# Chunk inverses of the first layer: one compact 64x64 tile per head in place of block-diagonal pairs

## The chip, the cores and the metric

The kernel runs on one core of a Trainium2 chip. The metric is the device time of one execution in microseconds. Three runs of the kernel before took 1829.59 to 1830.82 us, with a median of 1830.16 us.

## What is computed

The reference is a trunk of two layers on 256 tokens of width 1024. Layer 0 runs an RWKV-7 time mixer (8 heads of 64, both directions) beside an attention mixer, projects, and ends in a dense SwiGLU. Layer 1 runs a gated linear attention and a top-2-of-8 mixture of experts. The change touches only the recurrence of the RWKV-7 mixer:

```python
def step(state, inp):
    r_t, w_t, k_t, v_t, a_t, b_t = inp
    sa = jnp.einsum('bhvk,bhk->bhv', state, a_t)
    new = state * w_t[:, :, None, :] + sa[..., None] * b_t[:, :, None, :] + v_t[..., None] * k_t[:, :, None, :]
    read = state if reverse else new
    return new, jnp.einsum('bhvk,bhk->bhv', read, r_t)
...
_, out = lax.scan(step, init, xs, reverse=reverse)
```

The kernel does this scan in chunks of 64 tokens. In a chunk the `sa` of all tokens solve a triangular system of 64 unknowns for each head and direction; with its inverse at hand, the rest of the chunk is a few 64x64 products.

## The kernel before

All activations lie transposed, features on the partitions. 128 partitions hold two heads of 64 features (h = 0, 1); four such tiles (t, `RT` = 4) hold the eight heads, and two directions (d) double them. So each of the `NCH` = 4 steps of the chunk loop handles 16 systems, the list `SYSTEMS`; direction 0 takes chunk s and direction 1 chunk 3-s. The whole stage is one block of three engine programs (TensorE, ScalarE, VectorE) that order themselves by semaphores; SyncE issues nothing in it. Each engine executes its own list in the order in which it is written.

The steps are taken in pairs (s, s+1). The two members of a pair have a slot each (q = 0, 1) with its own tiles, and a pair goes through three parts.

- **Grams** (`grams`, L778 to L795, twice). TensorE forms for each of the 16 systems the products of decayed keys, values and queries in banks 0 to 4, and turns B, K and (first pair only) V into banks 5 to 7. VectorE masks bank 0 into X (L928), adds the identity (L935), forms XT from MT (L937, L938), and masks RB, AK and RK (L932, six instructions of 128x256). ScalarE copies MT (L883) and the turned tiles (L886). `grams(s+1)` may write a bank only once it has been taken from for step s.
- **Levels** (`levels`, L803 through `pairs_product`). The inverse of a unit triangular 64x64 matrix is built by doubling: X holds the inverse of the diagonal blocks of size b and XT its transpose; each of the five levels b = 2, 4, 8, 16, 32 multiplies M by X, masks the product with the level's mask (`masked_product`, L908), multiplies the masked product by X from either side, and adds what comes out to X and XT (`add_pairs`, L914). On the last level only XT is needed.
- **Recurrence** (`recur`, L832 to L854, twice): W, U, the new state and the output of the step, each a product of 64x64 per system, with copies by ScalarE (L890, L892) and sums by VectorE (L901, L903, L965 to L968).

In the levels, X, XT, MT and the masked product are stored as 8 tiles of 128x128: tile (d, t) has head 0's matrix in its upper left 64x64 block, head 1's in the lower right one, and zeros elsewhere. One matmul of 128x128 by 128 columns multiplies both heads at once. A product of a slot is 8 matmuls into two banks (one for each direction), and each VectorE pass over it takes two instructions of 128x512 elements. The zeros are written once, by two memsets of 128x3072 at the start of the block (L919); the first MT copy and VectorE itself wait for them. Since the blocks are written one head at a time, the X mask takes two instructions of 64x512 and the MT copy four of 64x256.

Within a level the written order is, on TensorE: M times X of slot 0, of slot 1, then both second products of slot 0, both of slot 1. On VectorE: mask of slot 0, mask of slot 1, adds of slot 0, adds of slot 1. A matmul of f32 operands leaves two MATMUL records (and two LDWEIGHTS records) in the trace, so that the 448 matmuls of `pairs_product` count as 896.

The block before this one ends at about 162 us with the attention mixer, the one behind it (L979 on) begins at about 347 us with the group norm and the output projection.

Of the kernel before, what the change touches and what calls it, by code (L numbers as in the profile page):

```python
# [7 lines left out]
P = 128  # L8
KT = D // P
TT = S // P  # L10
HD = 64
RW = 512
RT = RW // P
C = 64
# [73 lines left out]
def program(nc, io):  # L88
# [13 lines left out]
    with ctx:  # L102
# [590 lines left out]
        for q in range(2):  # L693
            at = TEMP_ + q * 3 * 1024
            slots.append({n: area(at + 1024 * j, 8, 2 * C) for j, n in enumerate(("X", "XT", "MT"))})
            at = TEMP_ + 8192 + q * 6 * 512
            slots[q].update({n: tile8(at + 512 * j) for j, n in enumerate(("AK", "RB", "RK", "Bt", "Kt", "Vt"))})
        product = [area(TEMP_ + 6144, 8, 2 * C), area(TEMP_ + 7168, 8, 2 * C)]
# [17 lines left out]
        def head_blocks(v, h):  # L716

            return v[HD * h:HD * (h + 1), :, C * h:C * (h + 1)]

# [5 lines left out]

        def by_direction(v):

            return v.rearrange("p (d t) (h n) -> p d (t h) n", d=2, h=2)

        def both_heads(name):  # L730
            return cst(name).rearrange("p (d n) -> p d n", d=2).unsqueeze(2).to_broadcast([P, 2, 2 * RT, C])

# [18 lines left out]
        eye = ident.unsqueeze(1).to_broadcast([P, 8, 2 * C])  # L751
        zeroed = sem("zeroed")

        with nc.Block(no_gpsimd_drain=True) as block:
            @block.tensor
            def _(pe):
# [42 lines left out]
                def pairs_product(bank, left, right):  # L799

                    for d in range(2):
                        for t in range(RT):
                            last = nc.tensor.matmul(ps[bank + d][:, t * 2 * C:(t + 1) * 2 * C], left[:, RT * d + t], right[:, RT * d + t],  # L803
                                                    start=True, stop=True)
                    return last

                def levels(s):
                    pe.wait_ge(grams_taken_dve, 4 * (s + 2))
                    pe.wait_ge(grams_taken_act, act_groups(s + 2))
                    for n in range(1, len(LEVELS)):  # L810
                        done = len(LEVELS) * (s // 2)
                        for q in range(2):
                            o = slots[q]
                            pe.wait_ge(inverse_ready[q], done + n)
                            pairs_product(4 * q, o["MT"], o["X"]).then_inc(product_ready[q], 1)
                        for q in range(2):
                            o = slots[q]
                            pe.wait_ge(product_masked[q], (len(LEVELS) - 1) * (s // 2) + n)
                            last = pairs_product(4 * q + 2, product[q], o["XT"])
                            if n < len(LEVELS) - 1:  # L820
                                last = pairs_product(4 * q, o["XT"], product[q])
                            last.then_inc(blocks_ready[q], 1)

                def recur(s):
# [11 lines left out]
                    for d, t, h in SYSTEMS:  # L836
                        p, j = slice(HD * h, HD * (h + 1)), RT * d + t
                        last = nc.tensor.matmul(bank8(5)[p, j], o["XT"][p, j, C * h:C * (h + 1)], W[p, j], start=True, stop=True)
# [29 lines left out]
            def _(act):  # L868
                for s in range(0, NCH, 2):
                    for q in range(2):  # L870
                        o = slots[q]
                        for n, (name, bank) in enumerate((("MT", 1), ("Bt", 5), ("Kt", 6), ("Vt", 7))):
# [3 lines left out]
                            if name == "MT":  # L876
                                act.wait_ge(grams_ready, gram_groups(s + q) + 3)
                                if s + q < 1:
                                    act.wait_ge(zeroed, 2)
                                for d in range(2):  # L880
                                    for h in range(2):
                                        rows = slice(HD * h, HD * (h + 1))
                                        last = nc.scalar.activation(head_blocks(o[name], h)[:, RT * d:RT * (d + 1)],  # L883
                                                                    side_by_side(1 + d)[rows, :, 0], ACT.Copy)
# [10 lines left out]
            def _(dve):  # L895
# [10 lines left out]
                def masked_product(q, d, name):  # L906
                    mask = cst(name)[:, d * C:(d + 1) * C].unsqueeze(1).to_broadcast([P, 2 * RT, C])
                    return nc.vector.tensor_tensor(product[q][:, RT * d:RT * (d + 1)].rearrange("p t (h n) -> p (t h) n", h=2),  # L908
                                                   bank8(4 * q + d), mask, mul)

                def add_pairs(v, bank):
                    for d in range(2):
# [1160 lines left out]
```

## Time and profile before

| | |
|---|---|
| median of three runs | 1830.16 us |
| profiled execution: span from the first to the last instruction | 1828.1 us |
| TensorE busy, whole span | 1694.6 us (93%) |
| VectorE busy, whole span | 1370.5 us (75%) |
| ScalarE busy, whole span | 1020.8 us (56%) |
| DMA queue 1, share of the 16 engines' span | 62.4% |

The page gives the profiled execution's span and no separate time around it; the median of the timed runs lies 2.1 us above that span. Busy times are sums over the instructions of an engine with overlaps counted once. A row of a group of instructions gives its busy time and the mean duration of one; as matmuls overlap in the array, the mean of one is much longer than the busy time divided by their number. "Idle" is the time in which the engine did nothing just before an instruction of the group, with the work that released it.

### The profile page before, as it was taken

How to read it: one execution, taken by the hardware profiler on the slowest of the kernel's cores; microseconds unless marked ns; L12 is line 12 of the kernel's file. 1: busy time of each engine (PE TensorE's matmuls, PEld its weight loads, DVE VectorE, ACT ScalarE, POOL GpSimd, SP SyncE). 2: the span in 40 equal slices, each digit the busy share in tenths (PEclk: the TensorE clock that was granted, in tenths of full speed). 3: DMA queues.
4: the chain of work that ended last, by engine and by line, in shares of the span. 5: the costliest groups of instructions: out<-in, count | busy, mean ns of one | idle time of the engine just before them, and what ended most of it. 6: DMA issues, size and time to landing. Idle time of an engine off the chain costs nothing. (4 is left out here: it accounts for less than half of the span.)

```text
span 1828.1 us, 35139 instructions
## 1 busy us (share of the span) xinstructions
PE 1694.6 (93%) x13430; PEld 1546.7 (85%) x13430; DVE 1370.5 (75%) x1861; ACT 1020.8 (56%) x1564; POOL 0.2 (0%) x4
## 2 busy tenths in 40 slices
PE   7967989689999896889999999999999999999997
PEld 6835979589999795879988898899889889898896
DVE  5678655565554576568888889889888898898885
ACT  4443010344442463357767677677677677676773
POOL 0000000000000000000000000000000000000000
PEclk9967999889999998899999999999999999999999
DMA  7200000045544340449989989899899899899892
GB/s 313 104 0 1 1 3 1 5 170 186 193 172 172 130 148 1 162 166 365 370 301 371 353 320 367 316 353 363 315 364 362 306 367 367 305 365 352 325 367 102
DMA packets 71952, 425.29 MB, mean 233 GB/s; under 512 B 8128, under 2 KB 8128, under 8 KB 37712
## 3 DMA queue, kind: packets, MB, share of 16 engines
q1 hardware_dynamic: 71888, 424.38, 62.4%
q8 instruction: 47, 0.77, 0.2%
q14 instruction: 17, 0.14, 0.0%
HBM read 423.30 MB, written 1.05 MB: 232 GB/s over the span
## 5 line engine op out<-in xcount | busy, mean ns | idle before, releaser
L152 DVE TENSOR_TENSOR w_low<-ring,w_high 128x1024 fp32r<-128x1024 f32 x801 | 951.4, 1220 | 172.2 <-ACT w_high L149 172.2
L149 ACT ACTIVATE w_high<-ring 128x1024 fp32r<-128x1024 f32 x801 | 810.8, 1052 | 100.0 <-PE bank L157 82.7
L155 PE MATMUL bank<-w_high,slots_high 128*96 128x256 f32 x1792 | 516.0, 288 | 1.2 <-DVE slots_low L152 1.2
L157 PE MATMUL bank<-w_high,slots_low 128*96 128x256 f32 x1792 | 500.7, 279 | 0.0
L156 PE MATMUL bank<-w_low,slots_high 128*96 128x256 f32 x1792 | 500.5, 279 | 0.0
L155 PEld LDWEIGHTS bank<-w_high,slots_high 128*96 128x96 f32 x1792 | 290.6, 162 | 17.9 <-issue 2.2
L156 PEld LDWEIGHTS bank<-w_low,slots_high 128*96 128x96 f32 x1792 | 289.4, 161 | 14.6
L157 PEld LDWEIGHTS bank<-w_high,slots_low 128*96 128x96 f32 x1792 | 290.1, 162 | 0.0
L155 PE MATMUL bank<-x_high,w_high 128*128 128x256 f32 x760 | 220.7, 290 | 32.1 <-PEq L975 11.6
L156 PE MATMUL bank<-x_low,w_high 128*128 128x256 f32 x760 | 219.2, 288 | 0.0
L157 PE MATMUL bank<-x_high,w_low 128*128 128x256 f32 x760 | 218.9, 288 | 0.0
L149 ACT ACTIVATE turned_high<-bank 128x96 fp32r<-128x96 f32 x224 | 56.4, 252 | 256.5 <-PE bank L1705 256.5
L155 PEld LDWEIGHTS bank<-x_high,w_high 128*128 128x128 f32 x760 | 150.0, 197 | 35.8 <-issue 34.6
L155 PE MATMUL bank<-w_high,turned_high 128*96 128x512 f32 x448 | 177.9, 397 | 0.7 <-DVE turned_low L152 0.7
L157 PE MATMUL bank<-w_high,turned_low 128*96 128x512 f32 x448 | 176.1, 393 | 0.0
L156 PE MATMUL bank<-w_low,turned_high 128*96 128x512 f32 x448 | 176.0, 393 | 0.0
L156 PEld LDWEIGHTS bank<-x_low,w_high 128*128 128x128 f32 x760 | 150.3, 198 | 0.0
L157 PEld LDWEIGHTS bank<-x_high,w_low 128*128 128x128 f32 x760 | 150.2, 198 | 0.0
L803 PE MATMUL bank<-scratch 128*128 128x128 f32 x896 | 104.3, 279 | 11.2 <-DVE scratch L914 6.3
L803 PEld LDWEIGHTS bank<-scratch 128*128 128x128 f32 x896 | 102.4, 194 | 13.0 <-DVE scratch L914 7.8
L157 PEld LDWEIGHTS bank<-w_high,turned_low 128*96 128x96 f32 x448 | 72.2, 161 | 31.3
L155 PEld LDWEIGHTS bank<-w_high,turned_high 128*96 128x96 f32 x448 | 72.5, 162 | 17.0 <-issue 1.0
(293 smaller groups left out, 1748.8 us busy)
## 6 DMA issues: line engine op xcount, KB each, us to landing
ring<-in_w_moe SPq DMA_DIRECT2D x224, 1024.0 KB, 7.1
ring<-in_w_moe SPq DMA_DIRECT2D x224, 512.0 KB, 7.2
ring<-in_w_ffn SPq DMA_DIRECT2D x22, 1536.0 KB, 6.4
ring<-in_w_in SPq DMA_DIRECT2D x15, 1536.0 KB, 6.6
ring<-in_w_out SPq DMA_DIRECT2D x6, 1536.0 KB, 6.4
scratch<-in_x SPq DMA_DIRECT2D x2, 512.0 KB, 4.2
out_y<-scratch SPq DMA_DIRECT2D x2, 512.0 KB, 2.6
const<-in_const SPq DMA_DIRECT2D x1, 948.0 KB, 13.0
```

The source lines that it names most:

```text
L149: return nc.scalar.activation(dst, src, ACT.Copy)
L152: return nc.vector.tensor_tensor(dst, src, high.bitcast(f32), sub)
L155: nc.tensor.matmul(out, left[0], right[0], start=start, stop=False, **flags)
L156: nc.tensor.matmul(out, left[0], right[1], start=False, stop=False, **flags)
L157: return nc.tensor.matmul(out, left[1], right[0], start=False, stop=stop, **flags)
L803: last = nc.tensor.matmul(ps[bank + d][:, t * 2 * C:(t + 1) * 2 * C], left[:, RT * d + t], right[:, RT * d + t], start=True, stop=True)
```

## The change

X, XT, MT and the masked product (now P, one of the slot's tiles) are stored like all the other tiles of a slot: 128x64 for each (d, t), head 0's matrix on partitions 0 to 63 and head 1's on 64 to 127. Nothing off the diagonal exists any more, so no zeros are written and nothing waits for them. A product is 16 matmuls of 64x64 by 64 columns into a single bank. Each VectorE pass over a slot's matrices is one instruction of 128x512; the identity added is that of 64x64. The MT copy is two instructions of 128x256.

```diff
-            at = TEMP_ + q * 3 * 1024
-            slots.append({n: area(at + 1024 * j, 8, 2 * C) for j, n in enumerate(("X", "XT", "MT"))})
-            at = TEMP_ + 8192 + q * 6 * 512
-            slots[q].update({n: tile8(at + 512 * j) for j, n in enumerate(("AK", "RB", "RK", "Bt", "Kt", "Vt"))})
-        product = [area(TEMP_ + 6144, 8, 2 * C), area(TEMP_ + 7168, 8, 2 * C)]
+            at = TEMP_ + q * 10 * 512
+            slots.append({n: tile8(at + 512 * j) for j, n in enumerate(("X", "XT", "MT", "P", "AK", "RB", "RK", "Bt", "Kt", "Vt"))})
...
-        eye = ident.unsqueeze(1).to_broadcast([P, 8, 2 * C])
-        zeroed = sem("zeroed")
+        eye = cst("ident64").unsqueeze(1).to_broadcast([P, 8, C])
...
-                def pairs_product(bank, left, right):
-
-                    for d in range(2):
-                        for t in range(RT):
-                            last = nc.tensor.matmul(ps[bank + d][:, t * 2 * C:(t + 1) * 2 * C], left[:, RT * d + t], right[:, RT * d + t],
-                                                    start=True, stop=True)
+                def head_products(bank, left, right):
+
+                    for d, t, h in SYSTEMS:
+                        p, j = slice(HD * h, HD * (h + 1)), RT * d + t
+                        last = nc.tensor.matmul(bank8(bank)[p, j], left[p, j], right[p, j], start=True, stop=True)
                     return last
...
-                            pairs_product(4 * q, o["MT"], o["X"]).then_inc(product_ready[q], 1)
+                            head_products(4 * q, o["MT"], o["X"]).then_inc(product_ready[q], 1)
...
-                            last = pairs_product(4 * q + 2, product[q], o["XT"])
+                            last = head_products(4 * q + 2, o["P"], o["XT"])
                             if n < len(LEVELS) - 1:
-                                last = pairs_product(4 * q, o["XT"], product[q])
+                                last = head_products(4 * q, o["XT"], o["P"])
...
-                        last = nc.tensor.matmul(bank8(5)[p, j], o["XT"][p, j, C * h:C * (h + 1)], W[p, j], start=True, stop=True)
+                        last = nc.tensor.matmul(bank8(5)[p, j], o["XT"][p, j], W[p, j], start=True, stop=True)
...
-                                if s + q < 1:
-                                    act.wait_ge(zeroed, 2)
                                 for d in range(2):
-                                    for h in range(2):
-                                        rows = slice(HD * h, HD * (h + 1))
-                                        last = nc.scalar.activation(head_blocks(o[name], h)[:, RT * d:RT * (d + 1)],
-                                                                    side_by_side(1 + d)[rows, :, 0], ACT.Copy)
+                                    last = nc.scalar.activation(o[name][:, RT * d:RT * (d + 1)], side_by_side(1 + d)[:, :, 0], ACT.Copy)
...
-                def add_pairs(v, bank):
-                    for d in range(2):
-                        w = v[:, RT * d:RT * (d + 1)].rearrange("p t n -> p (t n)")
-                        last = nc.vector.tensor_tensor(w, w, ps[bank + d][:, :], add)
-                    return last
-
-
-                for q in range(2):
-                    nc.vector.memset(area(TEMP_ + q * 3 * 1024, 3 * 1024), 0.0).then_inc(zeroed, 1)
-                dve.wait_ge(zeroed, 2)
+                def add_bank(v, bank):
+                    return nc.vector.tensor_tensor(v, v, bank8(bank), add)
+
...
-                        for h in range(2):
-                            p = slice(HD * h, HD * (h + 1))
-                            last = nc.vector.tensor_tensor(dirs(head_blocks(o["X"], h)), dirs(bank8(0)[p]), both("level1")[p], mul)
-                        last.then_inc(grams_taken_dve, 1)
+                        nc.vector.tensor_tensor(dirs(o["X"]), dirs(bank8(0)), both("level1"), mul).then_inc(grams_taken_dve, 1)
...
-                        dve_then(dve, nc.vector.tensor_tensor(by_direction(o["XT"]), by_direction(o["MT"]), both_heads("level1_t"), mul))
+                        dve_then(dve, nc.vector.tensor_tensor(dirs(o["XT"]), dirs(o["MT"]), both("level1_t"), mul))
...
-                            for d in range(2):
-                                last = masked_product(q, d, f"level{LEVELS[n]}")
-                            last.then_inc(product_masked[q], 1)
+                            nc.vector.tensor_tensor(dirs(slots[q]["P"]), dirs(bank8(4 * q)), both(f"level{LEVELS[n]}"), mul)\
+                                .then_inc(product_masked[q], 1)
...
                             if n < len(LEVELS) - 1:
-                                add_pairs(o["X"], 4 * q)
-                            add_pairs(o["XT"], 4 * q + 2).then_inc(inverse_ready[q], 1)
+                                add_bank(o["X"], 4 * q)
+                            add_bank(o["XT"], 4 * q + 2).then_inc(inverse_ready[q], 1)
```

No instruction changes its place relative to the others. What the diff does not show at a glance is the number and shape of VectorE's instructions. This is VectorE's list from the start of the block to the end of the first level, before (scratch is the working memory in which all tiles of the slots lie, bank a PSUM bank, const the masks and identities):

```order
L919 MEMSET scratch 128x3072 x2
L928 TENSOR_TENSOR scratch<-bank,const 64x8x64 x2
L935 TENSOR_TENSOR scratch<-scratch,const 128x1024
L937 TENSOR_TENSOR scratch<-scratch,const 128x1024
L938 TENSOR_TENSOR scratch<-scratch,const 128x1024
L932 TENSOR_TENSOR scratch<-bank,const 128x256 x6
...
L908 TENSOR_TENSOR scratch<-bank,const 128x512 x4
L914 TENSOR_TENSOR scratch<-scratch,bank 128x512 x8
```

And now, with the line numbers of the changed kernel:

```order
L892 TENSOR_TENSOR scratch<-bank,const 128x512
L898 TENSOR_TENSOR scratch<-scratch,const 128x512
L900 TENSOR_TENSOR scratch<-scratch,const 128x512
L901 TENSOR_TENSOR scratch<-scratch,const 128x512
L895 TENSOR_TENSOR scratch<-bank,const 128x256 x6
...
L913 TENSOR_TENSOR scratch<-bank,const 128x512 x2
L885 TENSOR_TENSOR scratch<-scratch,bank 128x512 x4
```

The two memsets are gone, one pass over a slot's matrices is half as many elements, and a level takes 6 instructions in place of 12.

## Rows read from the trace of the kernel before

**Rows 1.** The page: its span, and the granted clock in 40 slices.

```profile
span 1828.1 us, 35139 instructions
...
PEclk9967999889999998899999999999999999999999
```

**Rows 2.** Windows: stretch, length; busy PE, PEld, DVE, ACT, POOL; clock, DMA share, GB/s.

```profile
163.70:184.10 20.40, 16.89 (x378) 16.61 (x374) 19.41 (x24) 6.61 (x14) 0.00 (x0) 0.88 0.01 2
184.10:238.50 54.40, 51.20 (x448) 50.40 (x448) 33.66 (x54) 0.00 (x0) 0.00 (x0) 1.00 0.00 1
238.50:256.30 17.80, 14.43 (x450) 13.67 (x448) 4.67 (x9) 2.39 (x4) 0.00 (x0) 1.00 0.01 3
256.30:273.00 16.70, 13.02 (x320) 12.74 (x320) 14.37 (x23) 5.41 (x12) 0.00 (x0) 1.00 0.01 4
273.00:330.00 57.00, 53.82 (x477) 52.93 (x479) 34.45 (x56) 0.00 (x0) 0.00 (x0) 0.97 0.00 1
```

**Rows 3.** Groups of instructions, 163 to 346 us: busy us, mean ns, idle before.

```profile
L803 PE MATMUL bank<-scratch 128*128 128x128 f32 x896 | 104.3, 279 | 11.2 <-DVE scratch L914 6.3 <-DVE scratch L932 4.9
...
L914 DVE TENSOR_TENSOR scratch<-scratch,bank 128x512 f32<-128x512 f32 x72 | 44.8, 682 | 29.0 <-PE bank L803 29.0
L908 DVE TENSOR_TENSOR scratch<-bank,const 128x512 f32<-128x512 f32 x40 | 25.7, 684 | 14.5 <-PE bank L803 14.5
...
L932 DVE TENSOR_TENSOR scratch<-bank,const 128x256 f32<-128x256 f32 x24 | 8.3, 415 | 0.1
...
L883 ACT ACTIVATE scratch<-bank 64x256 f32<-64x256 f32 x16 | 6.0, 378 | 27.9 <-PE bank L788 15.8 <-DVE scratch L919 12.0
...
L919 DVE MEMSET scratch<- 128x3072 f32 x2 | 5.2, 2618 | 1.9 <-PEq L446 1.3 <-PE bank L788 0.6
L935 DVE TENSOR_TENSOR scratch<-scratch,const 128x1024 f32<-128x1024 f32 x4 | 4.9, 1225 | 0.1
```

**Rows 4.** Timeline, one level of the first pair: start us, length us, what, idle before.

```profile
209.47 10.98 PE L803 MATMUL bank<-scratch 128*128 128x128 f32 x96 [0.79 <-DVE scratch L914]
211.56 1.29 DVE L908 TENSOR_TENSOR scratch<-bank,const 128x512 f32<-128x512 f32 x2 [0.95 <-PE bank L803]
...
218.71 2.48 DVE L914 TENSOR_TENSOR scratch<-scratch,bank 128x512 f32<-128x512 f32 x4 [1.09 <-PE bank L803]
...
221.25 10.98 PE L803 MATMUL bank<-scratch 128*128 128x128 f32 x96 [0.79 <-DVE scratch L914]
```

**Rows 5.** Timeline, U of the first step: 16 matmuls of 64x64, their reader.

```profile
240.42 1.15 PE L838 MATMUL bank<-scratch 64*64 64x64 f32 x32 [0.70 <-ACT scratch L890]
241.62 0.60 ACT L892 ACTIVATE scratch<-bank 128x512 f32<-128x512 f32 x1 [1.25 <-PE bank L838]
```

**Rows 6.** Timeline, grams of the first pair: TensorE, and ScalarE's last copy.

```profile
170.17 2.97 PE L795 MATMUL bank<-const,scratch 64*64 64x64 f32 x96
...
172.97 1.11 PE L778 MATMUL bank<-scratch 64*64 64x64 f32 x32
...
175.64 3.71 PE L788 MATMUL bank<-scratch 64*64 64x128 f32 x64 [1.56 <-DVE scratch L932]
...
182.19 0.60 ACT L886 ACTIVATE scratch<-bank 128x512 f32<-128x512 f32 x1 [0.34 <-PE bank L795]
184.15 12.77 PE L803 MATMUL bank<-scratch 128*128 128x128 f32 x112 [2.00 <-DVE scratch L932]
```

**Rows 7.** Timeline, grams of the second pair: TensorE's two waits.

```profile
264.53 3.71 PE L788 MATMUL bank<-scratch 64*64 64x128 f32 x64 [0.54 <-DVE scratch L932]
...
273.04 4.26 PE L803 MATMUL bank<-scratch 128*128 128x128 f32 x24 [2.93 <-DVE scratch L932]
```

**Rows 8.** Windows of 1 us, columns as in rows 2: after two pauses of TensorE.

```profile
276.00:277.00 1.00, 1.00 (x7) 1.00 (x6) 0.92 (x2) 0.00 (x0) 0.00 (x0) 0.50 0.00 0
...
364.00:365.00 1.00, 0.78 (x3) 0.81 (x4) 0.00 (x0) 1.00 (x2) 0.00 (x0) 0.50 0.61 98
369.00:370.00 1.00, 1.00 (x7) 1.00 (x6) 0.00 (x0) 0.00 (x0) 0.00 (x0) 0.50 0.96 406
```

More of the change, by code:

```diff
@@ L714, in both @@
             return cst(name).rearrange("p (d n) -> p d n", d=2).unsqueeze(2).to_broadcast([P, 2, RT, C])
-        def head_blocks(v, h):
-            return v[HD * h:HD * (h + 1), :, C * h:C * (h + 1)]
         def dirs(v):
@@ L724, in bank8 @@
             return ps[b][:, :].rearrange("p (a n) -> p a n", n=C)
[L726 to L731, printed above, removed]
         def gram_groups(s):
@@ L904, in y_out @@
                     last.then_inc(y_taken, 1)
[L906 to L909, printed above, removed]
-                def add_pairs(v, bank):
-                    for d in range(2):
-                        w = v[:, RT * d:RT * (d + 1)].rearrange("p t n -> p (t n)")
-                        last = nc.vector.tensor_tensor(w, w, ps[bank + d][:, :], add)
-                    return last
-                for q in range(2):
-                    nc.vector.memset(area(TEMP_ + q * 3 * 1024, 3 * 1024), 0.0).then_inc(zeroed, 1)
-                dve.wait_ge(zeroed, 2)
+                def add_bank(v, bank):
+                    return nc.vector.tensor_tensor(v, v, bank8(bank), add)
                 for s in range(0, NCH, 2):
```

## The prediction

> **What bounds the kernel now.** I read the page first: TensorE is busy over almost all of the span of 1828.1 us, and the clock row shows where it ran slower [rows 1]. Then I cut the chunk stage out of the span and read it as windows [rows 2]. The reader is to see five stretches: grams of the first pair, its levels (54.4 us), its recurrence (17.8), grams of the second pair (16.7), its levels (57.0); a second recurrence follows. In the levels TensorE is busy 94% of the time, VectorE 62%, and nothing else runs. In the grams VectorE is the busier one (14.37 of 16.70 us against 13.02 in the second pair). DMA is idle throughout (share 0.01), no weights are loaded here, and the block ends with a barrier of all engines. So the stage is a serial piece of the kernel: a microsecond taken out of it moves all that follows by one. The median of the timed runs is 1830.2, 2.1 above the profiled span; I take the savings from the span's rows and subtract them from the median.
>
> The groups of the stage [rows 3] say that the 896 records of L803, 448 matmuls, are 104.3 us of TensorE and that it waits 11.2 us for VectorE around them. The timeline of one level [rows 4] says in which order: TensorE runs its 96 records without a break, then stands 0.79 us until VectorE's last add (218.71 + 2.48 = 221.19) releases it at 221.25. So a level is TensorE's work plus a short wait for VectorE.
>
> **A formula for a level, tried on the kernel before.** Write P for the time from the start of one product of a slot to the start of the next, A for the adds of a slot, t for the time from the last of the matmuls being issued to VectorE's start. The first product of slot 1 waits for the adds of slot 1, which start t after TensorE went over to the next level; then follow five P until slot 0's first product comes up again. The level is t + A + 0.06 + 5P. Before: a record lasts 275 ns and 96 take 10.98, so one is issued every (10.98 - 0.275) / 95 = 0.1127 us, and P = 16 x 0.1127 = 1.80. The adds start at 218.71, and 209.47 + 80 x 0.1127 = 218.48 (80 records: slot 1's first product and both pairs of second products), so t = 0.23. A = 2.48. Sum: 0.23 + 2.48 + 0.06 + 9.02 = 11.79 us. The trace has 221.25 - 209.47 = 11.78. The formula holds.
>
> **The level after.** P is now 16 matmuls of 64x64 by 64 columns, alternately on the upper and the lower half. The kernel does this already: L795's 96 records begin at 170.17 and the next group at 172.97 [rows 6], 0.0292 us a record, so P = 32 x 0.0292 = 0.93. L838, the same form with operands from the same memory, took 1.15 us for 32 records, and its reader started 1.20 after the first [rows 5]: t = 0.27. VectorE's instruction keeps its form (128x512, 682 to 684 ns, rows 3), but there are half as many: two back to back take 1.29 for the masks [rows 4], so A = 1.28 and a mask is 0.68. A level: 0.27 + 1.28 + 0.06 + 4.67 = **6.28 us** in place of 11.78. I checked that nothing else comes last: slot 0's mask is finished 0.4 us before TensorE wants it, slot 1's 0.9 us before, slot 0's adds 0.3 us before.
>
> A pair has four full levels, of which the first has no wait (6P = 5.60), and a last one with a single second product: 1.61 to slot 1's product, then P, P, P and 0.07 for a mask that is just late, 4.48. Sum 5.60 + 3 x 6.28 + 4.48 = 28.9 us; before, 54.4 [rows 2]. **Saved: 25.5 us a pair, 51.0 in all.**
>
> **Grams, first pair.** Removed: two memsets of 2.62 us [rows 3], for which ScalarE's first copy waited (12.0 us of idle time, most of it also the wait for the banks). Up to 172.97 + 1.1 = 174.0 TensorE waits for nobody, and that stays. What goes is its wait for VectorE: it stood 1.56 us before 175.64 and 2.00 before 184.15 [rows 6]. VectorE's chain for a slot was two instructions of 64x512 (taken at 0.69 like the wider ones), 3 x 1.23 and 2.08 (rows 3: six of L932, a quarter of 8.3), 7.1 us, and becomes 4 x 0.69 + 2.08 = 4.8 (the six masks L932 and their 2.08 us stay). It starts some 5 us earlier without the memsets, so step 0's chain is over before 174.0. What is late next is ScalarE: the last turned tile is copied in 0.60 us [rows 6] after TensorE's last gram, and levels wait for it; 0.69 with hops. VectorE's chain of slot 1 ends about 1 us before that. The MT copy is two instructions in place of four at 378 ns [rows 3], 0.76 in place of 1.54, on that chain and counted in it. Saved: 1.6 + 2.0 - 0.7 = **2.9 us**.
>
> **Grams, second pair.** TensorE waits 0.54 and 2.93 us [rows 7]. After: the first goes; of the second, VectorE's chain (bank ready, MT copy 0.76, two passes of 0.69, masks 2.08) ends at about the same time as ScalarE's last copy, 0.85 us behind TensorE. Saved: 0.54 + 2.93 - 0.85 = **2.6 us**.
>
> **The clock, second pair.** The second pair's levels took 57.0 us against 54.4 for the same work [rows 2]; the granted clock was 0.50 of full, the level of 1.2 GHz, in them [rows 8], behind the pause of 2.93 us. The pause of 2.00 us in the first pair was followed by no fall (1.00 in rows 2). With 0.85 us of pause I expect none: **2.6 us** saved. That is the term I am least sure of; its two ends are 0 and 2.6.
>
> **Recurrence:** XT is read from another address, same form, nothing changes. Instruction counts, addresses of the other tiles: nothing.
>
> **Sum:** 51.0 + 2.9 + 2.6 + 2.6 = 59.1 us. 1830.2 - 59.1 = **1771 us**.
>
> **Two rules against it.** The 64x64 products write both halves of one bank in turn. In the rows this costs nothing visible: L795 writes its bank just so, at 0.058 us a matmul [rows 6], where a 64-column matmul with a neighbour beside it on the other half is a quarter of the 0.225 us of a 128-column one. The Trainium skill, TensorEngine Tiling (Array Packing), section Restrictions and Gotchas, says that different row tiles cannot access the same PSUM bank at the same time, which would bar the overlap. By that rule the trace does not agree, and the result would be rival B.
>
> The second is on the clock: TensorE now pauses 0.68 us in every 6.28 instead of 0.96 in every 11.78 (0.79 as shown, plus the last record's own tail). In rows 2 the stretch from 238.5 to 273.0 has 64x64 work alone, TensorE busy 27.45 of 34.5 us, 80%, with pauses of 0.7 us, and the clock was 1.00. The Trainium skill, TensorE: Matmul & The Clock Gate, section A second HAM failure mode: psum-queue depth-cycling, says that frequent short idles between groups of matmuls make the clock swing between its levels. The trace does not show that here; it would be rivals A or C.
>
> **Rivals.**
> A, some levels run at 1.2 GHz. P would be 1.87 and, as that is longer than the wait of 1.6, a level 6P = 11.2: 4.9 us lost for each. Two to five levels give 1781 to 1796. For it: the fall behind 273 us. Against: the 1.00 in 238.5 to 273.0.
> B, neighbours do not overlap (the rule of the bank, or something in long runs of such matmuls that the short ones do not meet). At 0.117 us a matmul P is again 1.87, a level 11.2 against 11.78, a pair 4 x 11.2 + 4 x 1.87 = 52.3 against 54.4. Saved 4.2 + 5.5 + 2.6 = 12: 1818 us. The levels break even at 11.78 / 96 = 0.123 us. Against it: every 64x64 row at 0.058.
> C, on the other side: the clock falls and stays at 1.2 GHz through the whole stage, now that no full-array matmul is left in it. Levels as in B; but TensorE's 14.4 us of each recurrence, 13.0 of the second grams and some 10 of the first double: +52, less 12, so +40: 1870 us. It would decide from about 60% of the stage (59 of 99 us of difference) at the lower level. Against it are the same rows as for A.
> D, the change does not reach the end of the kernel: something later waits for a time of its own. The next block starts from a barrier, its weights lie in the ring, the DMA share is 0.01; I see nothing. 1830.
>
> **How the numbers follow.** Forecast 0.86, A 0.06, B 0.04, D 0.02, C 0.02. Own ends of the forecast: without any wait in the levels 8 x 0.68 = 5.4 us less, 1766; with the second pair's slow clock kept, 1774. Behind the stage TensorE restarts at 1.2 GHz and is still there at 369 to 370 us, some 6 us after it set in [rows 8], which costs 3 us; how long such a restart takes depends on when it falls, and all later ones shift, so 3 to 5 us either way. Range 1765 to 1779; it leaves out most of A, B, C and D. Faster by over 0.2% (3.7 us, about what a measurement of this kernel can tell from none): forecast, A, B: 0.96. Same 0.02, slower 0.02.
>
> **What would show it.** Right: the changed kernel has 1792 records of 64x64 in the levels with about 54 us busy, a level every 6.3 us, eight waits of TensorE for the adds, shown as about 0.5 us each (0.68 less a record's tail); levels of a pair 29 us; VectorE's groups of 128x512 at 682 ns, 36 and 20 of them; clock 1.00 from 170 to 287 us; next block at 288 us. Wrong: 0.058 becoming 0.1 or more with the clock at 1.00 (B); clock windows of 0.5 in the levels (A, C); a gap before the next block's first instructions (D); levels of 6.3 us at a gain under 50 us would mean that time was given back behind the stage.

## The result and the profile after

The changed kernel takes 1768.2 us (median of four runs, 1767.5 to 1769.8) against 1830.1 of the kernel before in the same comparison: a ratio of 0.9661, with a 95% interval of 0.9647 to 0.9675. It is 61.8 us faster; 59.1 were predicted, 1771 us in a range of 1765 to 1779.

The page of the kernel after, its head and its clock row; they answer to [rows 1]:

```profile
span 1766.2 us, 36860 instructions
...
PEclk9976998999999998899999999999999999999999
```

The windows of the stage, cut where its parts now begin; the columns are those of [rows 2]:

```profile
163.70:181.20 17.50, 16.77 (x389) 16.66 (x388) 9.52 (x20) 4.90 (x10) 0.00 (x0) 0.88 0.01 3
181.20:210.00 28.80, 26.98 (x897) 26.43 (x894) 17.89 (x28) 0.00 (x0) 0.00 (x0) 1.00 0.02 4
210.00:228.00 18.00, 14.37 (x457) 13.69 (x453) 3.92 (x8) 2.39 (x4) 0.00 (x0) 1.00 0.01 4
228.00:242.00 14.00, 13.26 (x343) 13.14 (x341) 9.52 (x20) 3.71 (x8) 0.00 (x0) 1.00 0.01 2
242.00:271.00 29.00, 27.18 (x903) 26.63 (x901) 18.22 (x28) 0.00 (x0) 0.00 (x0) 1.00 0.02 4
```

The levels are down from 54.4 and 57.0 us to about 29 each. TensorE is still busy 94% of them and VectorE 62%, as before: both halved. The clock is 1.00 in the levels and in the recurrence between them; in the grams VectorE (9.52 of 14.0 us) is no longer the busier engine.

The groups that answer to [rows 3] (busy us, mean ns, idle before, from 163 to 290 us):

```profile
L787 PE MATMUL bank<-scratch 64*64 64x64 f32 x1792 | 54.7, 219 | 5.1 <-DVE scratch L885 3.6 <-DVE scratch L895 0.7 <-issue 0.7
...
L885 DVE TENSOR_TENSOR scratch<-scratch,bank 128x512 f32<-128x512 f32 x36 | 23.3, 685 | 15.3 <-PE bank L787 15.3
...
L913 DVE TENSOR_TENSOR scratch<-bank,const 128x512 f32<-128x512 f32 x20 | 13.8, 689 | 9.1 <-PE bank L787 9.1
```

Twice the records of before in 54.7 us where there were 104.3: 0.0305 us a record, with the tail behind every burst counted in; within a burst it is 0.0293 (192 records in 5.81 us, the row below, less 0.22 for the last one's own length). VectorE's instructions kept their duration and are half as many.

One level of the first pair, which answers to [rows 4] (start, length, idle before):

```profile
187.69 5.81 PE L787 MATMUL bank<-scratch 64*64 64x64 f32 x192 [0.46 <-DVE scratch L885]
188.89 0.69 DVE L913 TENSOR_TENSOR scratch<-bank,const 128x512 f32<-128x512 f32 x1 [0.65 <-PE bank L787]
190.76 1.29 DVE L885 TENSOR_TENSOR scratch<-scratch,bank 128x512 f32<-128x512 f32 x2 [1.17 <-PE bank L787]
192.62 1.29 DVE L885 TENSOR_TENSOR scratch<-scratch,bank 128x512 f32<-128x512 f32 x2 [0.58 <-PE bank L787]
193.82 0.69 DVE L913 TENSOR_TENSOR scratch<-bank,const 128x512 f32<-128x512 f32 x1
193.97 5.81 PE L787 MATMUL bank<-scratch 64*64 64x64 f32 x192 [0.46 <-DVE scratch L885]
```

From 187.69 to 193.97 are 6.28 us. The last add begins at 192.62, lasts 1.29, and TensorE goes on at 193.97, 0.06 later: the chain of the prediction, wait included.

**Where the 61.9 us came from.** I cut each profiled execution in three, by the starts of two instructions: ahead of the stage (up to VectorE's last group before it, L541, at 161.08 before and 160.27 after), the stage (from there to the last of its outputs, L903 before, L881 after), and behind. The next row of each kernel is its last output, before at 346.42, after at 287.18:

```profile
346.42 0.75 DVE L903 TENSOR_TENSOR xn<-xn,bank 128x256 f32<-128x256 f32 x2 [6.83 <-PE bank L854]
```

```profile
287.18 0.75 DVE L881 TENSOR_TENSOR xn<-xn,bank 128x256 f32<-128x256 f32 x2 [6.83 <-PE bank L837]
```

| kernel | span | ahead | stage | behind |
|---|---|---|---|---|
| before | 1828.1 | 161.1 | 185.3 | 1481.7 |
| after | 1766.2 | 160.3 | 126.9 | 1479.0 |
| difference | -61.9 | -0.8 | -58.4 | -2.7 |

The profiled spans differ by 61.9 us. The stage gave 58.4 of them. The other 3.5 lie in code that is the same in both kernels; the experiments below come back to them.

### The profile page after: what moved, and what is told of

Its sections match the earlier page's. It is cut to its first block and busy times, and to the rows that moved or that the text cites. A ratio compares the mean times of both kernels' runs of the same rounds, so it can differ in the third digit from the quotient of the medians.

```text
span 1766.2 us, 36860 instructions
## 1 busy us (share of the span) xinstructions
PE 1639.9 (93%) x14326; PEld 1493.7 (85%) x14326; DVE 1322.1 (75%) x1799; ACT 1017.5 (58%) x1556; POOL 0.2 (0%) x4
## 5 line engine op out<-in xcount | busy, mean ns | idle before, releaser
L156 PEld LDWEIGHTS bank<-w_low,turned_high 128*96 128x96 f32 x448 | 72.2, 161 | 16.2
L1823 DVE TENSOR_TENSOR scratch<-scratch,bank 96x128 f32<-96x128 f32 x224 | 62.1, 277 | 7.7 <-ACT scratch L1745 7.7
```

What stands on the lines that cost most here:

```text
L156: nc.tensor.matmul(out, left[0], right[1], start=False, stop=False, **flags)
L1823: nc.vector.tensor_tensor(hidden_e[0:CAP, t % 2], silu_e[0:CAP, t % 2], ps[4 + t % 2][0:CAP, P:2 * P], mul)\
```

## The experiments

All are read by the same three parts; the whole table comes first, since most verdicts rest on it. "Behind" is the span less ahead and stage.

| kernel | median us | ahead | stage | behind |
|---|---|---|---|---|
| tensor_only | 1797.2 | 160.0 | 153.3 | 1481.7 |
| matmuls_twice | 1819.7 | 162.1 | 173.5 | 1482.1 |
| memsets_back | 1769.7 | 161.9 | 126.9 | 1478.9 |
| early_release | 1769.3 | 161.5 | 124.2 | 1481.6 |
| interleaved | 1767.6 | 160.7 | 122.6 | 1482.3 |
| heads_apart | 1801.9 | 159.8 | 155.7 | 1482.8 |
| pauses | 1778.4 | 160.2 | 134.3 | 1482.0 |
| early_in_before | 1826.1 | 160.4 | 180.6 | 1482.2 |
| delay8 | 1772.3 | 160.1 | 127.3 | 1481.8 |
| delay24 | 1773.8 | 160.0 | 128.2 | 1482.7 |
| delay58 | 1776.1 | 162.6 | 130.3 | 1481.0 |

**1. The matmuls alone (tensor_only).** The kernel before, with this edit:

```diff
-                    for d in range(2):
-                        for t in range(RT):
-                            last = nc.tensor.matmul(ps[bank + d][:, t * 2 * C:(t + 1) * 2 * C], left[:, RT * d + t], right[:, RT * d + t],
-                                                    start=True, stop=True)
+                    for d, t, h in SYSTEMS:
+                        p, j, n = slice(HD * h, HD * (h + 1)), RT * d + t, slice(C * h, C * (h + 1))
+                        last = nc.tensor.matmul(ps[bank + d][p, t * 2 * C + C * h:t * 2 * C + C * (h + 1)], left[p, j, n], right[p, j, n],
+                                                start=True, stop=True)
```

> The kernel before, with the matmuls of the change alone: 16 of 64x64 a product on the diagonal blocks, tiles and VectorE's instructions as before (the blocks off the diagonal hold numbers that nobody reads). My theory, a level is a chain through both engines: P = 0.93, adds 2.48, two masks 1.29 each; VectorE (7.5 us a level) becomes the bound with one hop to TensorE in its way: 8.3 us a level in place of 11.78, a pair's levels 38 us in place of 54.4, kernel about 1797 us. Rival, the gain is TensorE's alone and VectorE has room: levels 6.3 us, about 1779 us.

Measured: 1797.2 us (ratio 0.9817, 0.9799 to 0.9835), the stage 32.1 us shorter. The levels in VectorE's timeline:

```profile
197.00 4.87 DVE L914 TENSOR_TENSOR scratch<-scratch,bank 128x512 f32<-128x512 f32 x8 [0.84 <-PE bank L803]
201.79 2.62 DVE L908 TENSOR_TENSOR scratch<-bank,const 128x512 f32<-128x512 f32 x4
205.25 4.87 DVE L914 TENSOR_TENSOR scratch<-scratch,bank 128x512 f32<-128x512 f32 x8 [0.84 <-PE bank L803]
```

A level is 8.25 us (197.00 to 205.25); VectorE works 7.4 us of it without a pause but for 0.84, the hop through TensorE. The rival's 6.3 us is out: with cheap products and the old passes VectorE becomes the bound. The first pair's levels took 40.3 us from their first matmul to the first of the recurrence (183.03 to 223.35), the second pair's 38.1 (257.81 to 295.89), where 38 were expected for each; in the first pair the clock fell twice, to which experiment 7 comes back.

**2. Every matmul twice (matmuls_twice).** The changed kernel, with the compact passes but about TensorE's old amount of work:

```diff
-                    for d, t, h in SYSTEMS:
+                    for d, t, h in 2 * SYSTEMS:
                         p, j = slice(HD * h, HD * (h + 1)), RT * d + t
                         last = nc.tensor.matmul(bank8(bank)[p, j], left[p, j], right[p, j], start=True, stop=True)
```

> The changed kernel with every matmul of the levels issued twice (same result): P = 1.87, VectorE as changed. My theory: P is longer than the wait for the adds, so no wait is left and a level is 6P = 11.2 us; a pair's levels 52.3 us, kernel about 1768 + 47 = 1815 us, which says that VectorE's halving without the cheaper products is worth only about 0.6 us a level. Rival, VectorE's passes set the level: at most 5 us slower in all, under 1775 us.

Measured: the stage 46.6 us longer than after, with 47 expected. The total of 1819.7 is 4.7 over the expected one; the profiled execution took 1.8 us more ahead of the stage and 3.1 more behind it. The waits for VectorE's adds are gone:

```profile
L787 PE MATMUL bank<-scratch 64*64 64x64 f32 x3584 | 105.0, 218 | 1.5 <-DVE scratch L895 0.7 <-issue 0.7
```

VectorE's halving without the cheaper products is thus worth 185.3 - 173.5 = 11.8 us of stage, of which grams and clock are the larger part. 32.1 and 11.8 make 43.9; both together gave 58.4. The 11.8 is a little too low, because TensorE's work is a little more than before: a product takes 105.0 / 56 = 1.875 us here and took 1.80 before (56 products, 28 a pair). By my estimate that is 0.07 us in each of the 56 products, some 4 us, and the parts then make about 48. Each half of the change leaves the other engine as the bound, so the parts still don't add up to the whole.

**3. The memsets again (memsets_back).**

```diff
+                idle = area(TEMP_ + 10240, 3 * 1024)
+                for q in range(2):
+                    dve_then(dve, nc.vector.memset(idle, 0.0))
                 for s in range(0, NCH, 2):
```

> The changed kernel with two memsets of 128x3072 at the start of VectorE's program, into memory that nobody reads. My theory: in the new kernel TensorE is at 1.2 GHz and sets the first grams, VectorE's chain for step 0 has 5 us to spare, so they cost 0 to 0.5 us; what the change saved in the first grams came from the shorter passes. Rival, the memsets were on the path: +2.6 to +5.2 us.

Measured: the stage is 126.9 us, the same to the hundredth as after (126.91). The total is 1769.7 us, and the five runs of this one kernel lie between 1767.9 and 1774.5, so the total alone could not have told. The memsets cost nothing here: they have moved VectorE's first mask from 4.0 to 8.7 us behind the stage's start, and its chain still ends before TensorE asks for it. Their 5.2 us of busy time were no part of the gain by themselves.

**4. An earlier release (early_release).**

```diff
-                                add_bank(o["X"], 4 * q)
-                            add_bank(o["XT"], 4 * q + 2).then_inc(inverse_ready[q], 1)
+                                add_bank(o["X"], 4 * q).then_inc(inverse_ready[q], 1)
+                            last = add_bank(o["XT"], 4 * q + 2)
+                            if n == len(LEVELS) - 1:
+                                last.then_inc(inverse_ready[q], 1)
```

> The changed kernel, where TensorE's next product M times X is released after the add to X alone and no longer after the add to XT. By the formula level = t + A + 0.06 + 5P with A = 0.68: 1.01 + 4.67 = 5.68 us in place of 6.28, eight levels, -4.8 us: about 1763.5 us; idle time of TensorE before the levels' matmuls gone but for 0.1 us each. Rival, what TensorE waits for is something else than the last add (bank or queue): no change, 1768 us.

Measured: 1769.3 us (1767.8 to 1772.5) where 1763.5 were expected, no gain in the total; the stage is 2.7 us shorter and not 4.8. Neither theory holds. VectorE's timeline tells why:

```profile
187.55 1.28 DVE L885 TENSOR_TENSOR scratch<-scratch,bank 128x512 f32<-128x512 f32 x2 [0.58 <-PE bank L787]
188.75 1.43 DVE L913 TENSOR_TENSOR scratch<-bank,const 128x512 f32<-128x512 f32 x2
191.62 1.28 DVE L885 TENSOR_TENSOR scratch<-scratch,bank 128x512 f32<-128x512 f32 x2 [1.44 <-PE bank L787]
```

The mask of slot 0 starts at 188.75, right behind both adds of slot 1. TensorE's second product waits for it (188.75 + 0.68 + 0.06 = 189.49), and its own reader starts 2.13 later, at 191.62. The first wait had hidden a second one, for the mask, that is shorter by 0.3 us.

**5. The mask moved as well (interleaved).** The changed kernel with the early release, and with slot 0's mask ahead of slot 1's add to XT on VectorE:

```diff
+                    def mask_product(q, n):
+                        dve.wait_ge(product_ready[q], done + n)
+                        nc.vector.tensor_tensor(dirs(slots[q]["P"]), dirs(bank8(4 * q)), both(f"level{LEVELS[n]}"), mul)\
+                            .then_inc(product_masked[q], 1)
+
+                    mask_product(0, 1)
+                    mask_product(1, 1)
...
-                                add_bank(o["X"], 4 * q)
-                            add_bank(o["XT"], 4 * q + 2).then_inc(inverse_ready[q], 1)
+                            if not last_level:
+                                add_bank(o["X"], 4 * q).then_inc(inverse_ready[q], 1)
+                                if q:
+                                    mask_product(0, n + 1)
+                            last = add_bank(o["XT"], 4 * q + 2)
+                            if last_level:
+                                last.then_inc(inverse_ready[q], 1)
+                        if not last_level:
+                            mask_product(1, n + 1)
```

> early_release, and VectorE's mask of slot 0 moved ahead of the add to XT of slot 1. early_release left a level at 5.94 us where 5.68 was expected, because the mask of slot 0 stands behind both adds of slot 1 on VectorE and TensorE's second product waits for it. My theory: with the mask ahead a level is 5.68 us, the last one 0.36 us shorter too; the stage, from VectorE's last instruction before it to its last output, 122.6 us in place of 126.9 (changed kernel) and 124.2 (early_release). Rival, the 5.94 us come from TensorE itself (a slower record in an unbroken run): 124.2 us. In the timed runs it should be 1764 to 1767 us, since the parts before and behind the stage have moved by 2 to 3 us from run to run.

Measured: the stage takes 122.61 us, as expected, and a level 5.68:

```profile
192.59 0.69 DVE L885 TENSOR_TENSOR scratch<-scratch,bank 128x512 f32<-128x512 f32 x1 [0.58 <-PE bank L787]
...
198.27 0.69 DVE L885 TENSOR_TENSOR scratch<-scratch,bank 128x512 f32<-128x512 f32 x1 [0.58 <-PE bank L787]
```

This is the shortest stage of all, 4.3 us shorter than the changed kernel's and 1.6 shorter than with the early release alone. The whole kernel shows little of it: 1767.6 us (1767.1 to 1768.1) against 1768.2, just above the 1764 to 1767 expected, since the part behind took 3.2 us longer.

**6. The order of the heads (heads_apart).**

```diff
-                    for d, t, h in SYSTEMS:
+                    for h, d, t in [(h, d, t) for h in range(2) for d in range(2) for t in range(RT)]:
```

> The changed kernel with the matmuls of a product in another order: first the 8 of head 0 (upper half), then the 8 of head 1. Theory 1, two of them overlap only if neighbours stand on different halves: P = 1.8 to 1.87, levels as in matmuls_twice, stage 173 us, kernel about 1815 us. Theory 2, TensorE's queue lets matmuls of the two halves overlap wherever they stand, or the 0.058 us are no overlap at all: stage 127 us, kernel 1768 us.

Measured: 1801.9 us, the stage 28.7 us longer than after; the answer lies between the two theories.

```profile
L787 PE MATMUL bank<-scratch 64*64 64x64 f32 x1792 | 87.2, 221 | 1.5 <-DVE scratch L895 0.7 <-issue 0.7
```

A record takes 87.2 / 1792 = 0.0487 us in place of 0.0305, a matmul 0.097 in place of 0.061, counted in the same way. So the order of the list has a price, and the alternating order of `SYSTEMS` is worth about half of the change's gain (28.7 of 58.4 us). That neighbours on different halves overlap more than neighbours on the same half is my reading of the two rates; how far two of the same half still overlap is not shown. In any case a matmul in this order is cheaper than the 0.117 I had taken for neighbours without overlap.

**7. Pauses of TensorE (pauses).** The changed kernel, TensorE's and VectorE's side of it:

```diff
+                    pe.wait_ge(levels_start, s // 2 + 1)
                     for n in range(1, len(LEVELS)):
...
+                    nc.vector.memset(area(TEMP_ + 10240, 2560), 0.0).then_inc(levels_start, 1)
                     for n in range(1, len(LEVELS)):
```

> The changed kernel with a memset of 128x2560 on VectorE (about 2.2 us) ahead of the levels of each pair, for which TensorE waits, so that it pauses some 2.9 us there as it did before the second pair's levels in the kernel before. Theory 1, a pause of this length makes the clock fall: both pairs' first level runs partly at 1.2 GHz, 1 to 2 us lost each, stage 126.9 + 4.4 + 2 to 4 = 133 to 135 us. Theory 2, where the pause falls in time decides as well: one or neither of the two falls, 131 to 133 us.

Measured: the stage takes 134.3 us. TensorE paused 2.66 and 3.59 us, and the clock fell both times:

```profile
182.31 8.01 PE L788 MATMUL bank<-scratch 64*64 64x64 f32 x224 [2.66 <-DVE scratch L911]
...
246.82 8.16 PE L788 MATMUL bank<-scratch 64*64 64x64 f32 x224 [3.59 <-DVE scratch L911]
```

```profile
183.00:184.00 1.00, 1.00 (x25) 1.00 (x23) 0.00 (x0) 0.00 (x0) 0.00 (x0) 0.50 0.00 0
...
248.00:249.00 1.00, 1.00 (x25) 1.00 (x23) 0.17 (x1) 0.00 (x0) 0.00 (x0) 0.50 0.07 16
```

224 records take 8.01 and 8.16 us in place of 6.81: 1.2 and 1.35 us lost. This run alone speaks for theory 1. But tensor_only, which kept the old grams and so their pauses, had the falls the other way round from the kernel before. There TensorE stood 2.00 us ahead of the first pair and 2.93 ahead of the second, and the clock fell behind the shorter pause:

```profile
183.03 7.53 PE L803 MATMUL bank<-scratch 64*64 64x64 f32 x192 [2.00 <-DVE scratch L932]
```

```profile
186.00:187.00 1.00, 1.00 (x24) 1.00 (x22) 0.84 (x2) 0.00 (x0) 0.00 (x0) 0.50 0.00 0
...
258.00:259.00 1.00, 1.00 (x40) 1.00 (x39) 0.00 (x0) 0.00 (x0) 0.00 (x0) 1.00 0.00 0
```

At the same two lengths of pause the kernel before fell behind the longer one, tensor_only behind the shorter. (early_in_before, the next experiment, has the same two pauses and fell behind the longer one, as the kernel before did.) The length alone doesn't decide.

tensor_only shows one more fall, and there no long pause stands ahead of it. It came at 218.6 us, in the last level of the first pair:

```profile
213.00:218.00 5.00, 3.47 (x112) 3.19 (x108) 4.50 (x8) 0.00 (x0) 0.00 (x0) 1.00 0.01 3
...
220.00:221.00 1.00, 1.00 (x24) 1.00 (x22) 0.70 (x2) 0.00 (x0) 0.00 (x0) 0.50 0.00 0
```

```profile
216.03 1.15 PE L803 MATMUL bank<-scratch 64*64 64x64 f32 x32 [0.71 <-DVE scratch L914]
...
218.43 4.56 PE L803 MATMUL bank<-scratch 64*64 64x64 f32 x96 [1.24 <-DVE scratch L914]
```

TensorE had waited 0.71 and 1.24 us in each level and was busy 3.47 of the 5 us ahead. The second pair's levels have the same waits and no fall (mean clock 1.00 from 257.81 to 295.70). So a fall can come behind short waits too, and need not. In the changed kernel, with 0.46 us of wait in a level and TensorE busy 94% of it, there was none.

**8. The early release in the kernel before (early_in_before).** The edit of experiment 4 with `add_pairs`.

> The kernel before with the early release alone. By the chain with the mask of slot 0 behind both adds of slot 1 (2.71 + 1.29 to the second product): 3.98 + 4 x 1.80 = 11.2 us a level in place of 11.78, stage 185.3 - 4.7 = 180.6 us, and the clock may move that by 2 us. With my first formula, which leaves the mask out, a level would be 6P = 10.8 us and the stage 177.6 us.

Measured: 1826.1 us (ratio 0.9981, 0.9971 to 0.9991), the stage 180.6 us. The corrected chain, with the mask in it, gave 180.6; the first formula 177.6.

**9. Small delays (delay8, delay24, delay58).** N extra matmuls ahead of the second pair's levels, N = 8, 24, 58:

```diff
+                    for d, t, h in (4 * SYSTEMS)[:8] if s else ():
+                        p, j = slice(HD * h, HD * (h + 1)), RT * d + t
+                        nc.tensor.matmul(bank8(0)[p, j], slots[0]["MT"][p, j], slots[0]["X"][p, j], start=True, stop=True)
                     for n in range(1, len(LEVELS)):
                         done = len(LEVELS) * (s // 2)
```

> The changed kernel with 8 extra matmuls of 64x64 (0.47 us of busy TensorE, same result) ahead of the second pair's levels: everything behind comes 0.47 us later. The part of the kernel from the stage's last output to the end took 1479.0 us in the changed kernel and in memsets_back, 1481.6 to 1482.8 in the kernel before and in all six others. Theory 1, these 2.6 us are a matter of where in time the restarts of TensorE behind the stage fall, no merit of the change: the part behind can jump to 1481 or more although nothing in it is changed, and the kernel then gets 3 us slower by a delay of half a microsecond. Theory 2, they come from something the change did (its code, its memory, its instruction count): 1479.0 stays, and only the 0.47 us show.

> As delay8 with 24 extra matmuls, 1.40 us. Theory 1: the part behind lies anywhere from 1479 to 1483 us, and not at the same value in all three of these runs. Theory 2: 1479.0 us.

> As delay8 with 58 extra matmuls, 3.4 us. Theory 1: if the clock goes by periods of its own, a longer delay can bring the 1479 us back, so that this kernel may be no slower than delay8. Theory 2: 1479.0 us behind, 3.4 us slower in all.

Measured: with 0.4 us more of stage, delay8 takes 1772.3 us, 4.0 more than the changed kernel; its profiled span is 3.0 longer, 2.8 of it behind the stage. delay24 takes 1773.8 and delay58 1776.1, so the longest delay did not make the total as short as delay8's; its part behind is 1481.0 and not 1479. I cut the part behind once more, at the first scaled state of the gated linear attention in layer 1 (L1378 before, L1340 after). Windows from the stage's last output to there, before, after, and delay8, delay24, delay58 (columns as in [rows 2], the clock third from the end):

```profile
346.42:702.00 355.58, 324.50 (x2548) 312.63 (x2549) 200.96 (x248) 161.77 (x211) 0.00 (x0) 0.96 0.42 151
```

```profile
287.18:640.00 352.82, 321.19 (x2548) 309.71 (x2549) 200.84 (x248) 161.79 (x211) 0.00 (x0) 0.97 0.42 152
```

```profile
287.43:643.00 355.57, 324.62 (x2548) 312.73 (x2549) 200.92 (x248) 161.79 (x211) 0.00 (x0) 0.96 0.41 151
```

```profile
288.20:645.40 357.20, 325.92 (x2548) 313.64 (x2549) 200.81 (x247) 161.76 (x211) 0.00 (x0) 0.95 0.41 150
```

```profile
292.94:645.70 352.76, 321.13 (x2548) 309.68 (x2549) 200.80 (x247) 161.76 (x211) 0.00 (x0) 0.97 0.41 152
```

The same 2548 records of TensorE, the same work of the others, and 355.6, 352.8, 355.6, 357.2 and 352.8 us. The shorter time goes with the higher mean clock, 0.97 against 0.96 and 0.95. The difference lies in a few places where TensorE restarts; here are two of them, the first 30 us and the stretch from 250 to 290 us behind the last output, for the changed kernel and for delay8:

```profile
287.18:317.18 30.00, 16.48 (x99) 13.58 (x100) 19.40 (x27) 15.24 (x19) 0.00 (x0) 0.83 0.38 154
...
537.18:577.18 40.00, 35.31 (x235) 30.42 (x234) 19.91 (x25) 19.00 (x29) 0.00 (x0) 0.96 0.39 141
```

```profile
287.43:317.43 30.00, 16.48 (x89) 13.58 (x90) 18.54 (x26) 14.00 (x17) 0.00 (x0) 0.77 0.38 153
...
537.43:577.43 40.00, 35.31 (x226) 30.41 (x225) 21.16 (x27) 20.24 (x30) 0.00 (x0) 0.93 0.33 119
```

The same can be read in all thirteen traces. Up to layer 1 the clock stood at 1.2 GHz for 20.5 us in three of them (the changed kernel, memsets_back, delay58), and the stretch took 352.8 us; for 27.3 us in four (before, early_release, pauses, delay8), and it took 355.4 to 355.8; for 34.1 us in the other six, and it took 356.2 to 357.2. These times are added up from windows of 1 us; in a window with clock c the slow part is 2 x (1 - c).

So the 2.7 us are time at the slow clock. Theory 2 is out: early_release, interleaved and the delays all contain the change and do not all have them. That it matters where in time the stage ends (theory 1) fits the three delays, of which the first lost 2.8 us in this stretch, the second 4.4, and the longest none. It is less firmly shown, since each has one profiled execution, and in delay8 only 0.4 us of the shift is the delay: its last output stands 119.7 us behind the clock's rise in the first grams and the changed kernel's 119.1, of which 0.2 come from ahead of the stage. In delay58 the rest, from layer 1 on, took 1128.2 us in place of 1126.2; there too the clock was lower (0.98 against 0.99 over the last 368 and 366 us).

## Why the prediction was right

Each term of the sum against the two traces. The marks are TensorE's first matmul of the levels and ScalarE's first copy of W behind them: before 184.15 and 239.77 for the first pair, 273.04 and 331.26 for the second; after 180.43 and 210.58, 240.91 and 272.02.

| term | predicted | measured |
|---|---|---|
| levels, first pair | 25.5 | 55.62 - 30.15 = 25.5 |
| levels, second pair, and its clock | 25.5 + 2.6 | 58.22 - 31.11 = 27.1 |
| grams, first pair | 2.9 | 2.9 |
| grams, second pair | 2.6 | 2.9 |
| stage | 59.1 | 58.4 |
| outside the stage | 0, with 3 to 5 either way | 2.7 behind, 0.8 ahead |

**The level.** t + A + 0.06 + 5P gave 6.28 us, the trace has 6.28. Its prices came from matmuls and passes that the kernel before had already in the same form, which is why it came out so close. But the formula is right only where the last add comes last; it leaves out the mask of slot 0, which stands 0.4 us from the path in the changed kernel. I had noted that margin, and then forgot it in experiment 4. With the mask in the chain, interleaved (122.6) and early_in_before (180.6) came out as expected to the tenth.

**The clock term was mis-sized.** I took 57.0 - 54.4 = 2.6 us from two windows [rows 2], and the second one ended at 330, 0.9 us into the recurrence. Between marks of the same work the slow clock cost 58.22 - 55.62 = 2.6 of which the recurrence of the second pair's first step, which has 16 matmuls more for W, is 1.0; what is left is 1.6 (the distance from the first matmul to the first adds, 9.08 in place of 7.44 us, says 1.6 as well). In the difference of before and after the recurrence cancels: 27.1 - 25.5 = 1.6. So that term of the sum was 1.0 us too large. The reason given for it, a pause of 2.93 us that makes the clock fall where 2.00 does not, does not hold either: tensor_only fell behind 2.00 and not behind 2.93. That it did not fall in the changed kernel is in line with a pause of only 0.7 us and TensorE busy 94% behind it, but the fall in tensor_only at 218.6 us, behind a wait of 1.24, says that a short pause alone is no safety. The prediction also leaned on the stretch from 238.5 to 273.0 us as one with pauses of 0.7 us; the last 2.93 us of it are the long pause itself, and the fall came 1.4 us behind its end. That the clock would stay up was thus forecast on a reason that does not carry it, and there is luck in it.

**Grams.** Right, and the reason too: TensorE's waits of 1.56 and 0.54 us are gone, and 0.7 are left ahead of the levels of each pair. In the second pair I had taken 0.85 for what is left; that is 0.1 of the 0.3 us by which it gained more than forecast, and the rest stays open. memsets_back shows that the memsets were no part of it once the passes are short.

**The rivals.** B, serial neighbours, is ruled out by the trace after (0.061 us a matmul); heads_apart shows that a price of this kind exists, at 0.097 us and not at 0.117. The Trainium skill, TensorEngine Tiling (Array Packing), section Restrictions and Gotchas, has different row tiles barred from the same PSUM bank at the same time; here they write one bank in turn and are the cheaper for it, so the trace does not show the bar. A and C: the clock was 1.00 over all of the levels. The Trainium skill, TensorE: Matmul & The Clock Gate, section A second HAM failure mode: psum-queue depth-cycling, tells of a kernel in which frequent short idles make the clock swing. The changed kernel's trace does not show that: with a wait in each level, shown as 0.46 us, and only 64x64 matmuls there was no fall. The trace of tensor_only, with waits of 0.71 and 1.24 us in each level, has one fall in its levels at 218.6 us, so what rival A names does happen in a kernel of this kind. D: the next block followed as before; its first VectorE instruction starts 2.3 us behind the stage's last output in both kernels (348.69 and 289.46).

**Outside the stage.** The forecast had 3 to 5 us for the restarts behind the stage, either way. They gave 2.7 to the good side, and 0.8 more came from ahead of the stage, for which the forecast had nothing; so the total missed by 2.8 us although the stage missed by 0.7 the other way. The 2.7 us are time at the slow clock, as all thirteen traces show, and their sign was luck. The 0.8 us ahead are in the spread of that part over all runs (159.8 to 162.6). The stage's own 0.7 is a difference too: the clock term was 1.0 too large and the second grams 0.3 too small.

## What to carry to other kernels

A chain of short steps between two engines could be predicted here to the tenth of a microsecond, because every price was read from the same form of instruction in the trace; the one that missed followed only the step that came last and not every engine's written order. A change that halves the work of two engines at once can gain more than its parts (58.4 us against 43.9 here, or about 48 by the estimate above), because each alone leaves the other as the bound. Gains of 2 or 3 us in a kernel with pauses of TensorE should be read in the stage itself: the total can give or take as much by the later restarts alone.

## What I had not expected of the hardware

- 64x64 matmuls of f32 with 64 columns take 0.061 us if neighbours alternate between the halves of the array, and 0.097 if eight of one half follow each other (87.2 and 54.7 us for 1792 records): a factor of 1.6 from the order of a list, and not 2.
- The clock fell behind a pause of 2.00 us in one kernel and not behind one of 2.93 in the same run, and the other way round in the kernel before; behind a pause of 2.66 us it fell too. It even fell within a chain of waits of 0.71 and 1.24 us, TensorE busy 3.47 of the 5 us ahead, and not in the same chain of the second pair.
- The same code behind the stage, up to layer 1, took 352.8, 355.4 to 355.8, or 356.2 to 357.2 us, by whether the clock stood at 1.2 GHz for 20.5, 27.3 or 34.1 us of it. The kernel with a delay of 0.4 us had 27.3, the one with 3.4 us had 20.5 again.
